# Dense tokens of two expert layers in blocks of 32 tokens by 4 heads, half of them scored and searched from the middle of the queries on

## What is computed

```python
q = (xb @ w_query).reshape(-1, PEER_HEADS, 2, PEER_QHALF)        # 8 heads, 2 halves of 128
s = jnp.einsum('thpd,pkd->thpk', q, sub_keys)                    # 2 x 128 scores for a token and head
sv, si = lax.top_k(s, PEER_TOPK)                                 # 16 best of each half
cand = sv[:, :, 0, :, None] + sv[:, :, 1, None, :]               # 256 sums
top_s, top_p = lax.top_k(cand, PEER_TOPK)                        # 16 experts of 16384
g = jax.nn.softmax(top_s, axis=-1)
act = jax.nn.gelu(jnp.einsum('thkd,td->thk', u_tab[eidx], xb))
w = (g * act).astype(xb.dtype)
out = jnp.einsum('thk,thkd->td', w, v_tab[eidx])
```

## Time and profile before

| | |
|---|---|
| median of 3 runs | 1637.57 us (1636.19 to 1637.85) |
| the profiled execution | 1636.25 us, its span 1634.5 us |
| TensorE busy | 98% of the span |
| VectorE, ScalarE, GpSimd busy | 67%, 13%, 31% |
| mean granted TensorE clock | 0.997 |
| moved by DMA | 534.97 MB, 327 GB/s in the mean |

### The profile page before, as it was taken

The page is one execution under the profiler, slowest core; times in us unless marked ns, Lnnn a source line. Parts: engine busy times, 40 slices in busy tenths (PEclk is TensorE's granted clock), DMA queues, the critical chain, the costliest instruction groups (busy, mean ns, idle before and its releaser), DMA issues. The chain is left out here.

```text
span 1634.5 us, 30408 instructions
## 1 busy us (share of the span) xinstructions
PE 1599.5 (98%) x12244; PEld 1517.5 (93%) x12244; DVE 1090.1 (67%) x2433; ACT 212.6 (13%) x617; POOL 498.9 (31%) x423
## 2 busy tenths in 40 slices
PE   9999999999899999999999999999999999999997
PEld 7687899999899999998898888999999999999997
DVE  3362369998899998545436423999969989943441
ACT  2251221111011000000003312211211100000000
POOL 0000033336444456533300001233534434532310
PEclk9999999999999999999999999999999999999999
DMA  6303379999999999999983435899999999999991
GB/s 242 129 15 132 124 279 394 395 384 402 408 409 408 399 408 408 409 409 409 409 316 133 140 123 193 328 396 393 383 409 408 408 406 403 409 409 410 408 383 64
DMA packets 149981, 534.97 MB, mean 327 GB/s; under 512 B 17617, under 2 KB 20434, under 8 KB 149842
## 3 DMA queue, kind: packets, MB, share of 16 engines
q1 hardware_dynamic: 89938, 314.90, 50.2%
q0 software_dynamic: 59904, 218.13, 33.9%
HBM read 531.92 MB, written 1.05 MB: 326 GB/s over the span
## 5 line engine op out<-in xcount | busy, mean ns | idle before, releaser
L243 PE MATMUL ps<-big,raw 128*128 128x160 f32 (+2 forms) x5232 | 830.9, 320 | 3.4 <-ACT big L1131 3.1
L243 PEld LDWEIGHTS ps<-big,raw 128*128 128x128 f32 x5232 | 775.8, 191 | 43.9 <-issue 3.8
L1067 PE MATMUL ps<-big,raw 128*128 128x160 f32 x4096 | 579.0, 301 | 7.0 <-DVE big L1062 2.6
L1067 PEld LDWEIGHTS ps<-big,raw 128*128 128x128 f32 x4096 | 559.6, 190 | 16.2 <-DMA raw<-in_v_rows 12.9
L1091 POOL DMA_INDIRECT big<-in_u_rows,big x208 | 253.6, 1219 | 751.6 <-DVE big L1201 397.9
L1232 DVE SCALAR_TENSOR_TENSOR big<-big 128x1024 f32<-128x1024 f32 x201 | 258.0, 1284 | 190.5 <-PE ps L1067 114.5
L1091 POOL DMA_INDIRECT big<-in_v_rows,big x208 | 242.1, 1164 | 318.6 <-DVE big L1232 246.8
L1215 DVE CUSTOM_DVE_ANT_0 big<-big 128x1024 f32<-128x1024 f32 x208 | 244.3, 1221 | 24.1 <-DMA big<-in_u_rows,big 17.5
L1131 ACT ACTIVATE big<-ps 128x160 f32<-128x160 f32 x256 | 77.6, 304 | 512.2 <-PE ps L243 463.8
L1161 DVE MAX8 big<-big 128x8 f32<-128x128 f32 (+1 forms) x99 | 33.5, 339 | 103.0 <-ACT big L1100 91.1
L331 ACT ACTIVATE big<-h 128x272 f32<-128x272 f32 (+1 forms) x32 | 12.7, 420 | 647.5 <-DVE h L1306 597.3
(11 more groups left out here) (165 smaller groups left out, 717.9 us busy)
## 6 DMA issues: line engine op xcount, KB each, us to landing
raw<-in_u SPq DMA_DIRECT2D x256, 512.0 KB
raw<-in_v_rows SPq DMA_DIRECT2D x256, 512.0 KB
raw<-in_query SPq DMA_DIRECT2D x32, 512.0 KB
raw<-in_lru_w SPq DMA_DIRECT2D x24, 512.0 KB
raw<-in_mla_down SPq DMA_DIRECT2D x17, 512.0 KB
raw<-in_mla_out SPq DMA_DIRECT2D x8, 512.0 KB
big<-in_u_rows,big POOLq DMA_INDIRECT x208
big<-in_v_rows,big POOLq DMA_INDIRECT x208
```

Of the source, the lines that this page charges most:

```text
L243: mm = pe.matmul(out, w[:, c * P:(c + 1) * P], x[:, c, :], start=(c == 0), stop=(c == DC - 1))
L1067: return pe.matmul(accumulator(c), w, act_w[:, i, :], start=start, stop=False, skip_group_check=True)
```

## The change

The dense groups become blocks of 32 tokens by 4 heads too: 5 blocks (`DB`) by 2 halves of the heads, still 10 groups. Those of heads 0 to 3 are scored at product 8, with the gathered ones, 8 groups in all; 9 (layer 0) or 8 (layer 1) follow after product 15. The order of the finds is a list, `finds`: gathered groups 0 to 2, dense groups of the first half, then the other gathered and the other dense ones. A pair doesn't cross from one part to the next, so that each part of odd length ends in a find of one group. In layer 0 the widths are 2, 1, 2, 2, 1, 2, 2, 2, 2, 1, in layer 1 they are 2, 1, 2, 2, 1, 2, 1, 2, 2, 1: ten finds each, where there were 9 and 8. ScalarE copies a query product with one instruction for both kinds of blocks, and the masks of the spread have 4 heads where they had 8.

```diff
@@ peer(): layout
-    qt, at = take(0, (2, GD, PH, GT))
-    qg, at = take(at, (2 * GB, PH, LANES))
+    qg, at = take(0, (2 * (DB + GB), PH, LANES))
-    spread = spread.bitcast(BF16).rearrange("p (g w h k) -> p g w h k", w=SPREADS, h=PH, k=TOPK)
+    spread = spread.bitcast(BF16).rearrange("p (g w h k) -> p g w h k", w=SPREADS, h=HEADS_ABREAST, k=TOPK)
...
+    first_half = [*range(GB), *range(GG, GG + DB)]
+    second_half = [*range(GB, GG), *range(GG + DB, G)]
+    order = first_half + second_half
+    def pairs_of(first, last):
+        return [(k, min(2, last - k)) for k in range(first, last, 2)]
+    finds_of_rows = pairs_of(0, GB) + pairs_of(GB, GG)
+    finds = (pairs_of(0, GB) + pairs_of(GG, GG + DB) + pairs_of(GB, GG) + pairs_of(GG + DB, G))
...
@@ GpSimd
-                pool.wait_ge(rows_found, k // (2 * TOPK) + 1)
+                pool.wait_ge(rows_found, finds_until(k // TOPK))
...
@@ ScalarE
-                act.copy(qt[:, s % 2, :, n // 2:n // 2 + 1, :].rearrange("p g a t -> p g (a t)"),
-                         mem.ps[:, s % 2, 0:TD].rearrange("p (g t) -> p g t", t=GT))
...
-                         mem.ps[:, s % 2, TD:TB].rearrange("p (b t) -> p b t", t=LANES)).then_inc(st.free[s % 2], 1)
+                         mem.ps[:, s % 2, 0:TB].rearrange("p (b t) -> p b t", t=LANES)).then_inc(st.free[s % 2], 1)
                 if n == HALF_QUERY:
-                    for pos in range(GB):
+                    for pos in range(GB + DB):
                         take_scores(pos)
...
@@ VectorE
-                dve.wait_ge(scores_out, first + w)
+                dve.wait_ge(scores_out, order.index(first + w - 1) + 1)
...
-            for first in range(0, G, 2):
-                find(first, min(2, G - first))
-                if first:
+            for k, (first, w) in enumerate(finds):
+                find(first, w)
+                if k:
                     n = rows(n, n + ROWS_PER_FIND)
...
-            by_head = [P, GD, PH, TOPK]
+            by_head = [P, GD, HEADS_ABREAST, TOPK]
...
@@ TensorE
-                for b in range(GB):
-                    score(q * GB + b, [qg[:, half, b, heads, :].rearrange("p a t -> p (a t)") for half in range(2)])
+                for k, g in enumerate(at_once):
...
+                    score(q * len(first_half) + k, both)
...
-            for g in range(GD):
-                score(GG + g, [qt[:, half, g, :, :].rearrange("p h t -> p (h t)") for half in range(2)])
...
             for g in range(GD):
+                q, b = g // DB, g % DB
+                out = slice(q * HEADS_ABREAST * TOPK, (q + 1) * HEADS_ABREAST * TOPK)
                 for w in range(SPREADS):
-                    mm = pe.matmul(mem.ps[:, 2 + w, g * GT:(g + 1) * GT],
-                                   spread[:, g, w, :, :].rearrange("p h k -> p (h k)"), mem.token[:, :],
+                    mm = pe.matmul(mem.ps[out, 2 + w, b * LANES:(b + 1) * LANES],
+                                   spread[:, g, w, :, :].rearrange("p h k -> p (h k)"), mem.lanes[:, :],
```

More of the change, by code:

```diff
@@ L77 @@
 CON = {"iota": 0, "head": P, "token": P + PH, "freq": P + PH + GT, "sign": P + PH + GT + 1,
-       "eps": P + PH + GT + 2, "lane": P + PH + GT + 3}
-NCON = P + PH + GT + 3 + LANES
+       "eps": P + PH + GT + 2, "lane": P + PH + GT + 3, "abreast": P + PH + GT + 3 + LANES}
+NCON = P + PH + GT + 3 + LANES + HEADS_ABREAST
 def constants():
@@ L89, in constants @@
     con[:, CON["lane"]:CON["lane"] + LANES] = (p[:, None] % LANES) == np.arange(LANES)
+    con[:, CON["abreast"]:CON["abreast"] + HEADS_ABREAST] = (p[:, None] // LANES) == np.arange(HEADS_ABREAST)
     half = ROPE // 2
@@ L164, in __init__ @@
         self.vec = sb("vec", [P, NVEC])
-        self.token = sb("token", [P, GT], BF16)
+        self.lanes = sb("lanes", [P, LANES], BF16)
         self.ones = sb("ones", [P, P])
@@ L525, in _ @@
                             mem.con[:, 0:P].unsqueeze(2).to_broadcast([P, P, 2])).then_inc(iota_set, 1)
-            dve.tensor_copy(mem.token[:, :], mem.con[:, CON["token"]:CON["token"] + GT]).then_inc(iota_set, 1)
+            dve.tensor_copy(mem.lanes[:, :], mem.con[:, CON["lane"]:CON["lane"] + LANES]).then_inc(iota_set, 1)
             dve.wait_ge(iota_set, 2)
@@ L914, in peer @@
     TD = T - TG
-    GB, GD, NG = TG // LANES, TD // GT, TD // ST
+    GB, DB, NG = TG // LANES, TD // LANES, TD // ST
+    GD = DB * PH // HEADS_ABREAST
     EXTRA = TG % LANES // GT
@@ L941, in peer @@
     SPREADS = 2 + PARTS
-    spread, _ = take(SCATTER * TD, (GD * SPREADS * PH * TOPK // 2,))
-    spread = spread.bitcast(BF16).rearrange("p (g w h k) -> p g w h k", w=SPREADS, h=PH, k=TOPK)
+    spread, _ = take(SCATTER * TD, (GD * SPREADS * HEADS_ABREAST * TOPK // 2,))
+    spread = spread.bitcast(BF16).rearrange("p (g w h k) -> p g w h k", w=SPREADS, h=HEADS_ABREAST, k=TOPK)
     scores, at = take(SCATTER * TD, (G, 2 * NK))
@@ L970, in peer @@
     iota = mem.con[:, CON["iota"]:CON["iota"] + P]
-    head_mask = mem.con[:, CON["head"]:CON["head"] + PH]
+    head_mask = mem.con[:, CON["abreast"]:CON["abreast"] + HEADS_ABREAST]
     token_mask = mem.con[:, CON["token"]:CON["token"] + GT]
@@ L989, in peer, with finds_until @@
     HALF_QUERY = QUERIES // 2
+    first_half = [*range(GB), *range(GG, GG + DB)]
[5 more added lines that the diff above has]
+    finds = (pairs_of(0, GB) + pairs_of(GG, GG + DB) + pairs_of(GB, GG) + pairs_of(GG + DB, G))
+    def finds_until(group):
+        return 1 + max(k for k, (first, _) in enumerate(finds_of_rows) if first <= group)
     def weight_at(j):
@@ L1099, in take_scores @@
                 act.wait_ge(scored, pos + 1)
-                act.copy(scores[:, pos, :], mem.ps[:, 2 + pos % 4, 0:2 * NK]).then_inc(scores_out, 1)
+                act.copy(scores[:, order[pos], :], mem.ps[:, 2 + pos % 4, 0:2 * NK]).then_inc(scores_out, 1)
             for n in range(QUERIES):
@@ L1118, in _ @@
                         act.copy(reps[:, g, e * HW:(e + 1) * HW], mem.ps[:, TURN_BANK + e, :]).then_inc(reps_out, 1)
-            for pos in range(GB, G):
+            for pos in range(GB + DB, G):
                 take_scores(pos)
@@ L1198, in find @@
                 if first < GG:
-                    last = min(first + w, GG)
+                    last = first + w
                     step.wait(1)
@@ L1323, in score_rows @@
                 heads = slice(q * HEADS_ABREAST, (q + 1) * HEADS_ABREAST)
+                at_once = [first_half, second_half][q]
                 for r in range(2):
                     pe.wait_ge(st.free[r], (q + 1) * HEADS_ABREAST + 1)
-                for b in range(GB):
-                    score(q * GB + b, [qg[:, half, b, heads, :].rearrange("p a t -> p (a t)") for half in range(2)])
+                for k, g in enumerate(at_once):
+                    if EXTRA and g == GH:
+                        both = [qx[:, half].rearrange("p a t -> p (a t)") for half in range(2)]
+                    else:
+                        b = (g - GG) % DB if g >= GG else DB + g % GB
+                        both = [qg[:, half, b, heads, :].rearrange("p a t -> p (a t)") for half in range(2)]
+                    score(q * len(first_half) + k, both)
             for n in range(QUERIES):
@@ L1345, in _ @@
             score_rows(1)
-            if EXTRA:
-                score(GH, [qx[:, half].rearrange("p a t -> p (a t)") for half in range(2)])
-            for g in range(GD):
-                score(GG + g, [qt[:, half, g, :, :].rearrange("p h t -> p (h t)") for half in range(2)])
             def u_product(i):
```

## The result

The changed kernel takes 1640.99 us (median of 20 runs, 1637.55 to 1644.91), the kernel before 1636.63 us (20 runs, 1633.75 to 1637.85): ratio 1.0027, 95% interval 1.0020 to 1.0034. It is slower, by 4.4 us (0.27%); 1633.1 us was predicted, and the range (to 1639.0) doesn't hold it. The profiled execution took 1639.8 us, its span is 1638.0 us, 3.5 us longer than before.

What follows compares the result with a forecast made beforehand. Layer 0 was taken to end when its bytes have come (DMA), layer 1 when its matmuls are done (TensorE). -8.9 + 4.3 + 0.1 = -4.5 us from 1637.6 gave 1633.1 us, range 1627.5 to 1639.

Steps and rivals of the forecast that it cites:

- Layer 0's -8.9 us: Layer 0, TensorE: 4.1 us earlier chain plus 7.7 less DMA, minus 2.4 for tiles and 0.5 for one-group cycles.
- The 7.7 us for six row steps that were done earlier: Layer 0's v phase: six fewer row steps left, each 1.28 us of DMA at 409 GB/s, 7.7 us less to come.
- layer 0 ends when its bytes have come: Layer 0's v phase: bound by DMA, a tile and one gather needing 2.56 us at 409 GB/s.
- earlier rows don't shorten layer 0's end: Rival, chance 0.14: DMA can't take early gathers or tiles fall back; only 4.1 us of layer 0's gain stays, 1637.9 us.
- The 4.1 us of VectorE's earlier chain: Layer 0: VectorE's chain of finds and row steps ends at 380.9 instead of 385.0 us, 4.1 us earlier.
- the fourth rival: Chance 0.06: the early find doesn't start and the hole stays in part; at a quarter, 3 us per layer, 1637.3 us.
- The third rival: Chance 0.14: cycles of one group wait for their rows, in both layers; 1645.7 us at 3.0 us per gather.
- Layer 1's +4.3 us: Layer 1, TensorE: chain ends 7.1 us later, giving a new 2.5 us wait at the gates plus a 1.8 us clock drop.
- The wait of 2.5 us: Layer 1: TensorE's new wait before the first product of gates, 1.9 to 3.0 us, taken as 2.5.
- the clock drop: Layer 1: one drop of TensorE's clock after the new wait, 1.8 us; called a matter of luck.
- The spread counted at nothing: From finds to casts, both layers: some 3.6 us less masked multiply work gives nothing, since VectorE waits for rows.
- Scores +0.1 us: Scoring as 8 and 9 or 8 groups instead of 3 and 14: 0.1 us more in layer 1, nothing in layer 0.

Runs made afterwards that it cites:

- six small gathers: Kernel before, with 6 gathers of layer 0's v phase replaced by 4 KB copies (those rows' values left out of the result): 1635.11 us, ratio 0.9993.
- the 24: Kernel before, with 24 gathers of layer 0's v phase, every third, replaced by 4 KB copies: 1622.24 us, ratio 0.9913.
- the edit in layer 0 alone: Changed kernel without the 6 row steps behind the second find in layer 0; layer 1 keeps them: 1635.35 us, ratio 0.9993.
- kernel before with five: Kernel before, with 5 row steps behind each find instead of 6, in both layers: 1652.03 us, ratio 1.0090.
- the run with the late second find: Changed kernel, but the second find waits until all groups are scored, undoing the early start: 1664.33 us, ratio 1.0173.
- the run with two queues: Changed kernel, with every second v tile from tile 21 to 127 fetched by ScalarE's DMA queue instead of SyncE's: 1645.86 us, ratio 1.0058.

## Why the prediction was wrong

- **Layer 0's -8.9 us: wrong, +0.1 us. Two steps failed.** *The 7.7 us for six row steps that were done earlier* were the larger part. This failed step alone nearly decides it: by the prediction's own sum, a chain that is only 0.2 us earlier would still have left a gain of 0.2 + 7.7 - 0.1 - 0.5 = 7.3 us. The rows in the prediction were right (2.52 us for a tile, 409 GB/s, 12.9 us of waits), the conclusion "layer 0 ends when its bytes have come" was not: the tiles' half of the DMA ends it, as long as the gathers have work but aren't the last. 1.28 us per gather assumes that one queue's saved bytes go to the other; six small gathers show no gain. The 13.1 us of the 24 (841.87 against 855.00) are the whole 12.9 us of waits for tiles, which by bytes too would be all there is to gain, so it is the run with six that decides. The rival "earlier rows don't shorten layer 0's end", which had chance 0.14, was right on these 7.7 us, though for neither of its reasons (the DMA took the early gathers in, and from 224 to 640 us TensorE has no wait for a tile); the 4.1 us that it left standing did not come either.
- *The 4.1 us of VectorE's earlier chain* was the other. The chain's arithmetic holds: 380.9 plus the wait of 3.46 us is 384.4, measured 384.81; and without the wait and six row steps it is 374.68. What failed was the assumption that the six rows are there in time: the last comes 18.5 us after the first find, and a find of one group with five row steps is over before that. This is what the fourth rival (chance 0.06) says in so many words, "the first rows haven't landed when the second find ends", at the quarter of the hole for which it gave numbers: 3.46 us of 13.53. It put layer 0 at -7.7 us with it, since it too priced the six rows at 7.7. The third rival, waits in every cycle of one group, did not happen: in the profile the later ones don't wait. In layer 1 the wait at this place is 0.28 us.
- **Layer 1's +4.3 us: right in mechanism, and near in size, in part by luck.** 3.4 us in the profiled execution, 5.7 us in the one with the edit in layer 0 alone, the slowest of its 11. VectorE's chain is 8.9 us later instead of 7.1, of which 0.28 us is a wait for rows. The wait of 2.5 us and the clock drop are in the run with the edit in layer 0 alone; in the changed kernel the 1.54 us and the two gaps stand in for the wait. Why TensorE stands still in one execution and hardly in the other I haven't tested. What the tiles got doesn't tell: from 1160 to 1190 us 6.98 MB before, 6.46 in the changed kernel, 6.34 with the edit in layer 0 alone, and 6.37 without those row steps in both layers, where TensorE doesn't stand still at all.
- **The clock.** Of the drop I had said that it can't be read beforehand; 2.46 us went with 0.91. A wait of TensorE for VectorE at the start of layer 0's v phase shows that the size of a gap alone doesn't decide: 2.23, 2.30 and 2.34 us (without row steps behind the second find in both layers; kernel before with five; without them in layer 0 alone) left the window at 1.00, and 2.33 us in the run with the late second find went with 0.91 from 540 to 560 us.
- **The spread counted at nothing: right** in the changed kernel (43.65 and 43.2 us from shift to casts, 43.3 and 44.4 before). **Scores +0.1 us:** u tiles of layer 1 start 0.27 us later; nothing rests on it.
- **The sum.** Layer 0 gives 0 for -8.9 and layer 1 costs 3.4 for 4.4: 3.5 us more span. The medians say 4.4. The profiled execution of the kernel before lies 0.4 us below its median, that of the changed one 1.2 us below; that makes up the rest.

The change as such is good: with its early start and without the row steps behind the second find, the kernel gains 6.1 us; with five row steps per find, 4.6 us. What made it slower is that six row steps stayed behind every find, while the finds became more and shorter.

## What to carry to other kernels

Where two queues saturate the DMA, price a transfer by its own queue's share: bytes saved in one queue are worth nothing to the other until that queue runs dry, and what a queue doesn't ask for while its slots are full goes to the other and, in these runs, did not come back. When a change gives an engine a free stretch, ask what the rule that hangs work on each step (here six row steps per find) puts into it, and tune that number again before judging the change.

## What the runs showed of the hardware

The two queues shared to within 0.1% over 106 us (21.62 and 21.60 MB). The last gathers of the run with two queues, with next to nothing beside them, moved 254 GB/s in 5 us, 0.62 of the ceiling of 409; that is the end of a queue, and no run shows gathers alone for longer. And a first group of rows takes long: the sixth is in the buffers only at 223.97 us, 18.5 us after the find behind which its gather could start (the second find begins at 205.43), 3.1 us for each in the mean, at 339 GB/s in all from 205 to 224 us. That is more than the hole that the change closed: in the kernel before, the first rows were fetched while VectorE was idle.
